# Up pass of a Strassen-like MLP: one 512-column matmul for the high and low activations, and the two halves of the bank added when it is read

## The reference, cut to what matters

```python
h = h + mixed @ w_out[l]
u = rms_norm(h, norm_mlp_g[l])
h = h + jnp.square(jax.nn.relu(u @ w_mlp_up[l])) @ w_mlp_down[l]
return rms_norm(h, norm_final_g)
```

## Time and profile before

| | |
|---|---|
| Time before, median of 3 runs | 2671.78 us (2670.11 to 2671.96) |
| The profiled execution | 2670.39 us, its span 2668.6 us |
| TensorE clock granted, mean | 0.992 |
| PE busy | 2599.9 us, 97% of the span |
| DVE, ACT, POOL busy | 1653.1, 1149.5, 470.3 us |

### The profile page before, as it was taken

How to read it: one execution, slowest core, us unless ns; L and a number is a source line. 1 busy time by engine, 2 the same in 40 slices (tenths; PEclk the granted TensorE clock), 3 DMA queues, 4 the chain that set the end, 5 groups by cost and what they waited for, 6 DMA issues and landing times.

```text
span 2668.6 us, 37358 instructions
## 1 busy us (share of the span) xinstructions
PE 2599.9 (97%) x14116; PEld 2245.1 (84%) x14116; DVE 1653.1 (62%) x1665; ACT 1149.5 (43%) x1429; POOL 470.3 (18%) x320
## 2 busy tenths in 40 slices
PE   7999999999999999999979999999997999999998
PEld 6777878888888888888879999999996788888886
DVE  4436855433333332342377777777777899999996
ACT  4323345412232232232355565556554455555555
POOL 1000010000000000000002223223322343434343
PEclk9999999999999999999999999999998999999999
DMA  4222222222222222234335655665568565445651
GB/s 172 80 94 79 95 98 96 81 95 93 89 84 80 79 95 94 94 111 139 128 111 184 213 195 177 205 207 177 193 213 328 206 229 195 177 186 219 236 205 79
DMA packets 247375, 394.41 MB, mean 148 GB/s; under 512 B 8832, under 2 KB 156880, under 8 KB 238864
## 3 DMA queue, kind: packets, MB, share of 16 engines
q1 hardware_dynamic: 243024, 378.17, 41.2%
q0 software_dynamic: 3344, 9.96, 1.1%
q10 hardware_dynamic: 944, 5.42, 0.5%
HBM read 326.28 MB, written 67.11 MB: 147 GB/s over the span
## 4 chain that ended last, share of the span: by engine, by line
PE 69%; issue 22%; POOL 5%; DMA 2%; DVE 2%; ACT 1%; POOLq 0%; DVEq 0%; ACTq 0%; SPq 0%
PE stream L1529 15%; PE stream L1531 15%; PE stream L1530 15%; PE aux L1827 4%; PE aux L1829 4%; PE aux L1828 4%; POOL hs L575 3%; PE stream L1829 3%; PE stream L1828 3%; PE stream L1827 3%; POOL hs L578 1%; DMA d<-in_w_mlp_down 1%; DMA sums_d<-hlo 1%; PE aux L1709 1%; PE aux L1529 0%
## 5 line engine op out<-in xcount | busy, mean ns | idle before, releaser
L1035 DVE TENSOR_TENSOR wlo<-raw,whi 128x2048 fp32r<-128x2048 f32 (+1 forms) x113 | 258.1, 2284 | 541.4 <-ACT whi L634 541.3
L1529 PE MATMUL stream<-uhi,whi 128*128 128x512 f32 (+1 forms) x1312 | 513.4, 391 | 1.5 <-ACT rx L704 0.8
L1531 PE MATMUL stream<-uhi,wlo 128*128 128x512 f32 (+1 forms) x1312 | 507.6, 387 | 0.0
L1530 PE MATMUL stream<-ulo,whi 128*128 128x512 f32 (+1 forms) x1312 | 507.6, 387 | 0.0
L634 ACT CAST whi<-raw 128x2048 fp32r<-128x2048 f32 (+1 forms) x113 | 215.3, 1906 | 534.3 <-PE stream L1531 533.7
L598 POOL TENSOR_TENSOR hh<-hh,dn_tmp 128x512 f32<-128x512 f32 x124 | 237.0, 1932 | 373.2 <-ACT dn_tmp L954 373.2
L1529 PEld LDWEIGHTS stream<-uhi,whi 128*128 128x128 f32 (+1 forms) x1312 | 245.1, 187 | 58.9 <-issue 7.5
L1531 PEld LDWEIGHTS stream<-uhi,wlo 128*128 128x128 f32 (+1 forms) x1312 | 245.0, 187 | 50.6
L1530 PEld LDWEIGHTS stream<-ulo,whi 128*128 128x128 f32 (+1 forms) x1312 | 245.2, 187 | 49.3 <-issue 1.0
L1791 PE MATMUL stream<-shi,uwhi 128*128 128x256 f32 x896 | 255.5, 285 | 10.1 <-DVE slo L1307 10.1
L1792 PE MATMUL stream<-slo,uwhi 128*128 128x256 f32 x896 | 254.4, 284 | 0.0
(11 more groups left out here) (254 smaller groups left out, 5191.9 us busy)
## 6 DMA issues: line engine op xcount, KB each, us to landing
raw<-in_w_in SPq DMA_DIRECT2D x80, 1024.0 KB, 5.0
d<-in_w_mlp_down SPq DMA_DIRECT2D x64, 1024.0 KB, 8.1
dsum<-sums_d SPq DMA_DIRECT2D x56, 1024.0 KB, 8.0
up_a<-in_w_mlp_up SPq DMA_DIRECT2D x32, 1024.0 KB, 6.1
up_b<-in_w_mlp_up SPq DMA_DIRECT2D x32, 1024.0 KB, 8.4
sums_d<-hhi SPq DMA_DIRECT2D x32, 896.0 KB, 5.3
sums_d<-hlo SPq DMA_DIRECT2D x32, 896.0 KB, 7.1
raw<-in_w_out SPq DMA_DIRECT2D x16, 1024.0 KB, 5.1
```

The source lines that it names most:

```text
L1035: V.tensor_tensor(wlo[slot][:, 0:width], raw[slot][:, 0:width], whi[slot][:, 0:width].bitcast(F32), ALU.subtract).then_inc(s.lo_ready, 1)
L1529: T.matmul(dst, ah, bh, start=first and k == 0, stop=False)
L1530: T.matmul(dst, ah, bl, start=False, stop=False)
L1531: ins = T.matmul(dst, al, bh, start=False, stop=last and k == n - 1)
```

## The change

High and low activation sums of one chunk come to lie in one tensor with a dimension of two (`ssum[q][:, c, j]`, c = 0 high, 1 low). PE multiplies `wh` by both in one matmul of 512 columns: high x high lands in the left half of the bank, high x low in the right half. `wl*sh` still has 256 columns and adds to the left half. A step now has 8 matmuls of 512 and 8 of 256 columns.

The value of a bank is left half + right half, and the sum is made where the bank is read. ACT copies the **right** half (semaphore `up_right`), and DVE adds the left half to the copy in a new `whole`, which raises `up_snap`. The two banks that `hid_out` reads itself take one more DVE add each (`up_half` orders the two). The relu on the end value is now an ACT instruction of its own over `c21`. PE's waits on `up_snap` stay as written.

```diff
-    shi = [at(f"shi{k}", a, [P, 7, HALF], F32R) for k, (a, _) in enumerate(sum_at)]
-    slo = [at(f"slo{k}", b, [P, 7, HALF], F32R) for k, (_, b) in enumerate(sum_at)]
+    sums_near = {k: at(f"sums{k}", kb, [P, 2, 7, HALF], F32R) for k, kb in ((0, 112), (1, 126), (2, 176), (7, 32))}
+    sums_far = at("sums_far", 48, [P, 2, 4, 8, HALF], F32R)
+    ssum = [sums_near[k][:] if k in sums_near else sums_far[:, :, k - 3, 0:7] for k in range(8)]
...
# ACT, up_act (a, c, a_old are now the columns HALF:S of the banks)
-                    nc.scalar.copy(snap["U3"][:], a_old).then_inc(s.up_snap, 1)
+                    nc.scalar.copy(snap["U3"][:], a_old).then_inc(s.up_right, 1)
                 if j == 3 and not first:
-                    nc.scalar.activation(c21[:], a_old, ACT.Relu).then_inc(s.up_snap, 1)
+                    nc.scalar.copy(c21[:], a_old).then_inc(s.up_right, 1)
...
# ACT, hid_act
             act.wait_ge(s.up_snap, 5 * i + 5)
+            nc.scalar.activation(c21[:], c21[:], ACT.Relu).then_inc(s.up_relu, 1)
             if begun:
                 act.wait_ge(s.hs_add, 4 * i)
+            act.wait_ge(s.up_relu, 2 * i + 2)
             nc.scalar.activation(h21[:], c21[:], ACT.Square).then_inc(s.up_sq, 1)
-            act.wait_ge(s.up_relu, i + 1)
...
# DVE, up_dve, ahead of the uwlo subtract of step j
+                if j >= 4:
+                    whole(i, j - 4, u)
+                if j in (1, 3) and not first:
+                    whole(i - 1, j + 3, u - 1)
...
# DVE, hid_out
+            V.tensor_tensor(up_out[:, x, 0:HALF], b[:, 0:HALF], snap[part][:], op).then_inc(s.up_half, 1)
+            if j == 2:
                 V.tensor_tensor(up_out[:, 2, 0:HALF], snap["Q5"][:], snap["U3"][:], ALU.subtract).then_inc(s.up_c, 1)
+            dve.wait_ge(s.up_half, 2 * i + j // 2 + 1)
+            V.tensor_tensor(up_out[:, x, 0:HALF], up_out[:, x, 0:HALF], b[:, HALF:S], ALU.add).then_inc(s.up_c, 1)
+
+        def whole(i, k, u):
+
+            part = (snap["P1"], snap["Q5"], snap["U2"], None, snap["U3"], None, c21)[k][:]
+            dve.wait_ge(s.up_right, 5 * i + {0: 1, 1: 2, 2: 3, 4: 4, 6: 5}[k])
+            V.tensor_tensor(part, up_bank(u, k)[:, 0:HALF], part, ALU.add).then_inc(s.up_snap, 1)
...
# PE, up_pe
-                    T.matmul(dst, wh, sh, start=opens and q == 0, stop=False, skip_group_check=not opens)
-                    T.matmul(dst, wh, sl, start=False, stop=False, skip_group_check=not opens)
-                    ins = T.matmul(dst, wl, sh, start=False, stop=q == KP - 1, skip_group_check=not opens)
+                    if q:
+                        T.matmul(dst[:, 0:HALF], wl, sh, start=False, stop=False, skip_group_check=True)
+                    ins = T.matmul(both, wh, hl, start=opens and q == 0, stop=q == KP - 1, skip_group_check=True)
+                    if q == 0:
+                        T.matmul(dst[:, 0:HALF], wl, sh, start=False, stop=False, skip_group_check=True)
```

More of the change, by code:

```diff
@@ L173, in __init__ @@
         self.up_mm = nc.alloc_semaphore("up_mm")
+        self.up_right = nc.alloc_semaphore("up_right")
+        self.up_half = nc.alloc_semaphore("up_half")
         self.up_snap = nc.alloc_semaphore("up_snap")
@@ L846, in sum_hi @@
             act.wait_ge(s.st_add, 4 * k + 4)
-            nc.scalar.copy(shi[k][:], hs[k % 2][:]).then_inc(s.st_hi, 1)
+            nc.scalar.copy(shi[k], hs[k % 2][:]).then_inc(s.st_hi, 1)
         def squares(c):
@@ L879, in up_act @@
                     act.wait_ge(s.up_c, 3 * i)
-                    nc.scalar.copy(snap["U3"][:], a_old).then_inc(s.up_snap, 1)
+                    nc.scalar.copy(snap["U3"][:], a_old).then_inc(s.up_right, 1)
                 if j == 3 and not first:
-                    nc.scalar.activation(c21[:], a_old, ACT.Relu).then_inc(s.up_snap, 1)
+                    nc.scalar.copy(c21[:], a_old).then_inc(s.up_right, 1)
                 if j == 4:
                     act.wait_ge(s.up_c, 3 * i + 1)
-                    nc.scalar.copy(snap["P1"][:], a).then_inc(s.up_snap, 1)
+                    nc.scalar.copy(snap["P1"][:], a).then_inc(s.up_right, 1)
                 if j == 5:
                     act.wait_ge(s.up_c, 3 * i + 3)
-                    nc.scalar.copy(snap["Q5"][:], c).then_inc(s.up_snap, 1)
+                    nc.scalar.copy(snap["Q5"][:], c).then_inc(s.up_right, 1)
                 if j == 6:
                     act.wait_ge(s.up_c, 3 * i + 2)
-                    nc.scalar.copy(snap["U2"][:], a).then_inc(s.up_snap, 1)
+                    nc.scalar.copy(snap["U2"][:], a).then_inc(s.up_right, 1)
                 if j < len(hooks):
@@ L966, in dn_act @@
                     act.wait_ge(s.up_c, 3 * PAIRS)
-                    nc.scalar.copy(snap["U3"][:], up_bank(3, 0)[:, 0:HALF]).then_inc(s.up_snap, 1)
+                    nc.scalar.copy(snap["U3"][:], up_bank(3, 0)[:, HALF:S]).then_inc(s.up_right, 1)
                 if first and m == 3:
-                    nc.scalar.activation(c21[:], up_bank(3, 0)[:, 0:HALF], ACT.Relu).then_inc(s.up_snap, 1)
+                    nc.scalar.copy(c21[:], up_bank(3, 0)[:, HALF:S]).then_inc(s.up_right, 1)
                 if m == 2 and not first:
@@ L1364, in hid_out @@
         def hid_out(i, u, j):
+            dve.wait_ge(s.up_mm, 7 * i + 8 + j)
+            x, part, op = ((0, "P1", ALU.add), None, (1, "U2", ALU.subtract))[j]
+            b = up_bank(u, 3 + j)
+            dve.wait_ge(s.up_snap, 5 * i + {0: 1, 2: 4}[j])
             if j == 0:
-                dve.wait_ge(s.up_mm, 7 * i + 8)
-                dve.wait_ge(s.up_snap, 5 * i + 1)
                 dve.wait_ge(s.up_sq, 2 * i + 2)
-                V.tensor_tensor(up_out[:, 0, 0:HALF], up_bank(u, 3)[:, 0:HALF], snap["P1"][:], ALU.add).then_inc(s.up_c, 1)
-            else:
-                dve.wait_ge(s.up_mm, 7 * i + 10)
-                dve.wait_ge(s.up_snap, 5 * i + 4)
-                V.tensor_tensor(up_out[:, 1, 0:HALF], up_bank(u, 5)[:, 0:HALF], snap["U2"][:], ALU.subtract).then_inc(s.up_c, 1)
-                V.tensor_tensor(up_out[:, 2, 0:HALF], snap["Q5"][:], snap["U3"][:], ALU.subtract).then_inc(s.up_c, 1)
+            V.tensor_tensor(up_out[:, x, 0:HALF], b[:, 0:HALF], snap[part][:], op).then_inc(s.up_half, 1)
+            if j == 2:
+                V.tensor_tensor(up_out[:, 2, 0:HALF], snap["Q5"][:], snap["U3"][:], ALU.subtract).then_inc(s.up_c, 1)
+            dve.wait_ge(s.up_half, 2 * i + j // 2 + 1)
[4 more added lines that the diff above has]
+            V.tensor_tensor(part, up_bank(u, k)[:, 0:HALF], part, ALU.add).then_inc(s.up_snap, 1)
         def hid_lo(i):
@@ L1470, in dn_dve @@
                     add(3, dn_e[hf][:], b11, b21)
+                if first and m in (1, 3):
+                    whole(PAIRS - 1, m + 3, 3)
                 dve.wait_ge(s.dn_hi, 14 * st + m + 1)
@@ L1786, in up_pe @@
                     pe.wait_ge(s.up_snap, 5 * i + {2: 1, 4: 3, 5: 2, 6: 4}[j])
-                dst = up_bank(u, j)[:, 0:HALF]
+                dst = up_bank(u, j)
+                both = dst[:].rearrange("p (c n) -> p c n", c=2)
                 opens = j in (0, 1, 3)
                 for q in range(KP):
-                    wh, wl, sh, sl = uwhi[k][:, q], uwlo[k][:, q], shi[q][:, j], slo[q][:, j]
-                    T.matmul(dst, wh, sh, start=opens and q == 0, stop=False, skip_group_check=not opens)
-                    T.matmul(dst, wh, sl, start=False, stop=False, skip_group_check=not opens)
-                    ins = T.matmul(dst, wl, sh, start=False, stop=q == KP - 1, skip_group_check=not opens)
+                    wh, wl, hl, sh = uwhi[k][:, q], uwlo[k][:, q], ssum[q][:, :, j], shi[q][:, j]
+                    if q:
[3 more added lines that the diff above has]
+                        T.matmul(dst[:, 0:HALF], wl, sh, start=False, stop=False, skip_group_check=True)
                 ins.then_inc(s.up_mm, 1)
```

8 lines of the change are left out of this document (4 added, 4 removed).

## The result

The changed kernel takes 2775.33 us, median of 4 runs (2773.81 to 2777.21); the kernel before took 2670.95 us on the same chip (4 runs, 2667.6 to 2671.96). The ratio is 1.0397 [1.0384, 1.041]: slower by 104 us.

The account below looks back on a forecast made before the run. PE was taken to bound the up pass at 20.2 us per pair, with a chain beside it 0.3 us short of binding. 30 x (4.1 loop + 1.3 clock) + 5 ends = 167 us slower, 2838 us; range 2788 to 2880.

Parts of the forecast that it names:

- The wait that moves: PE's step 6 waits for U3's `whole` in DVE's next step 1, closing a loop of 24.3 us, 4.1 more per pair.
- Copy to the end of the second weight sum: Loop term from ACT's U2 copy to DVE's second weight sum, taken from the trace before the change: 12.57 us.
- Rival 4: Short loop: POOL's sums end before step 6's cast, 21.2 us per pair, clock unaffected, 2704 us; chance 0.05.
- The second half of P1's result: Loop term on DVE: the extra add in `hid_out` with its wait on the first half, +0.62 us per pair.
- the ends: First pair, last pair and the later down pass start, taken together as 5 us more (bounds 3 and 7).
- The clock: PE's clock falls to half around the 4.9 us gap ahead of step 6: 1.3 us per pair (bounds 0 and 2.1).
- Rival 1: The loop closes at U3 but PE's clock holds: 127 us slower, 2799 us; chance 0.18.
- PE's gain: Merged matmuls make PE's steps 2.77 instead of 2.88 us, 0.8 us less per pair, 26 us if PE stayed the bound.
- the ring: Chain `hhi`, `hlo`, DVE's list, step 4's cast, squares, POOL's sums, next `hhi`; forecast saw 0.3 us to spare beside PE.
- Rival 3: No change: U3 no hindrance, `uwlo` of step 0 binds at 20.2 us per pair, 2671 us; chance 0.02.
- By load alone DVE is no bound: DVE's seven more adds, 2.3 to 2.6 us, make 18.3 us busy per pair, which fits in 19.4.
- ACT's new relu: Separate relu on `c21` ahead of the squares, at most 0.4 plus 0.2 us, taken as hidden by PE's steps 1 and 2.

Follow-up runs that it names:

- The bare hand-over: Kernel before, with ACT's U3 copy signalling DVE, which raises `up_snap` where U3's `whole` would stand, no work added: 2675.33 us.
- the run with POOL's sums cut: Kernel before with merged matmuls, right half never read, and POOL's four sums replaced by one of 64 columns and three fills: 2651.52 us.
- the four that ran: Changed kernel with U3's `whole` moved forward, 2709.81 us; also P1's `whole` to step 3, 2719.82; U3's behind P1's result, 2719.16; `hid_act` earlier on the first of these, 2710.14.

## Why the prediction was right in direction and too large in size

*The wait that moves: right.* U3's `whole` behind `hlo` and both weight sums closes a loop through PE's step 6. The profile after shows the wait at that line in 31 pairs, moving the add gives back 66 us, and one operation at the same place in the kernel before makes the wait by itself.

*Copy to the end of the second weight sum, 12.57 us "as in the trace": the step that failed.* The stretch was carried over whole. It contained 4.79 us from U2's copy to `hhi`, which was no chain of its own but the distance between two: `hhi` came when POOL's four sums were done, and these began 1.75 us ahead of the copy and took 6.5 us, the first two of them beside a DVE that paused only once, for 0.38 us, up to 1706.96. After the change DVE waits for its hand-overs, and its adds have an operand in PSUM; the sums take 3.9 us and `hhi` comes 2.02 us behind the copy: 2.77 less. The bare hand-over, with pauses of DVE and no new operation, has the same 3.9 us, so the pauses are enough for it. I had seen the effect, but took off 0.4 us for it (0.7 at the low end), by the one sum that had been drawn out after 1706.96; I did not redo POOL's stretch for the DVE of the changed kernel. Rival 4, the short loop, went by this mechanism with 21.2 us; the loop itself is 22.2. Its cast behind step 6's weights at no wait was nearly true (0.70 us of wait), but its chance was 0.05 and it had no loss of clock.

*The rest of the loop, per pair.* The second half of P1's result added 0.45 instead of 0.62. Steps of 2.80 instead of 2.77 make 0.13 more, hand-overs of 0.4 instead of 0.15 (22.2 - 10.6 - 4 x 2.80) 0.25 more. The clock took 1.55 instead of 1.3. From the full sum of 24.74 us: 24.74 - 2.77 - 0.17 + 0.13 + 0.25 = 22.18, with the clock 23.73; measured 23.76. This closes by its making, since the hand-overs and the clock's part are what was left of measured distances. Against 24.3 + 1.3 = 25.6 it is 1.84 us less in each of 30 pairs, 55 of the 63 us by which the forecast was too high. Most of the rest lies in the ends, priced at +5: the first pair was 0.6 us shorter instead, and outside the stretch from the first to the last U2 copy, which grew by 105.8 us, the span grew by only 0.3. One slip besides: the low end of 2788 leaves out the 1.4 us that the other figures have; with them it is 2790.

*The clock: right that it falls, and nearly in size, in part by luck.* 3/4 x 1.7 mixed a chance with a length, for gaps of 4.9 us where 2.4 came; in fact it fell in 28 of 30 pairs and cost 1.55 each. Filling the gap gives it back, 42 us. Rival 1 fails by this.

*PE's gain: right in sign, smaller.* 0.6 us per pair instead of 0.8. The Trainium skill's constant of 2.5 ns per matmul ("TensorE: Matmul & The Clock Gate", section "Back-to-back issue gap") gave 5 us for the whole merge; the run with POOL's sums cut measures 20, so the trace sides with the rows. By itself the merge gains nothing: the ring of 20.2 us stood ready, as the run of the merge alone shows. Rival 3 named its end, `uwlo` of step 0, and its 20.2 us, but reckoned them with three steps of PE, which the ring doesn't hold; that the number fits is luck.

*"By load alone DVE is no bound": right of DVE, wrong of the kernel.* The seven adds fit in DVE's time, but some of them lengthen the ring. Seven operations much like them, at the same places in the kernel before and without the hand-over, cost 29 us. In the changed kernel itself the ring doesn't bind: ACT waits 1.54 us for PE ahead of P1's copy.

*ACT's new relu: hidden*, as said: POOL's first sum starts 1.96 us ahead of the U2 copy.

Two things stay open. How the 104 us divide between loop, load and clock can't be given as a sum, since each changes the others: POOL cut short gives 68.5, the clock 42, the move of U3 66. And whether an order exists in which both loops and the ring are under 19.6 us was not settled; the four that ran did not show one.

## What to carry to other kernels

When a buffer's release moves to another engine, walk the whole way from the releasing instruction's place in that engine's list back to itself, then do it again for each other release: with the first loop opened, the second stood 1.3 us above the old pair. A stretch taken from a trace holds the contention of its neighbours; if the change gives a neighbour pauses or takes them, do the stretch over. A gap in PE is paid twice if the clock falls behind it: here gaps of 1.1 to 1.6 us cost their own time, and gaps of 2.35 us nearly always 1.55 us more, so the last microsecond of a gap can be worth more than its own time says.
